# The softmax probabilities of the odd heads are transposed on VectorE instead of TensorE

## The reference

```python
s = jnp.einsum('bkgqd,bksd->bkgqs', qblk, k).astype(jnp.float32) * scale
p = jax.nn.softmax(s, axis=-1).astype(v.dtype)
return jnp.einsum('bkgqs,bksd->bkgqd', p, v)          # self-attention, 8 heads
...
mp = jax.nn.softmax(ms, axis=-1).astype(mv.dtype)
mo = jnp.einsum('bhqm,bhmd->bhqd', mp, mv)             # cross-attention, 4 heads
...
y = (g[:, :, 0] * (y_sgu @ w_br_sgu) + g[:, :, 1] * (y_attn @ w_br_attn) + g[:, :, 2] * (y_mem @ w_br_mem))
x = x + y @ w_out
```

## Time and profile before

| | us |
|---|---|
| median of 3 runs | 2754.28 |
| the profiled execution's own time | 2754.83 |
| its span, first to last instruction | 2753.0 |
| TensorE busy | 2745.2 |
| VectorE busy | 1728.5 |
| ScalarE busy | 1242.9 |
| GpSimd busy | 43.5 |

### The profile page before, as it was taken

One profiled execution on the slowest core, in us unless ns is written; L12 is line 12 of the kernel. 1 busy time (PEld: TensorE's weight loads), 2 busy tenths in 40 slices (PEclk: granted clock), 3 DMA queues, 4 the chain that ended last, 5 costly groups with the idle time before them and its releaser, 6 DMA issues.

```text
span 2753.0 us, 29833 instructions
## 1 busy us (share of the span) xinstructions
PE 2745.2 (100%) x12274; PEld 2276.1 (83%) x12274; DVE 1728.5 (63%) x2110; ACT 1242.9 (45%) x1395; POOL 43.5 (2%) x60
## 2 busy tenths in 40 slices
PE   9999999999999999999999999999999999999999
PEld 7888888888888888888888888888888888888887
DVE  7775555565666576656766755555657665765665
ACT  6545444444444344434454454444444443444343
POOL 0001000000000000000000010000000000000000
PEclk9999999999999999999999999999999999999999
DMA  9544455655555556555555545555555555555554
GB/s 366 188 183 161 180 204 195 212 187 183 185 199 198 192 191 228 191 192 199 190 179 184 181 157 184 194 205 200 178 189 184 199 197 188 197 184 199 186 205 143
DMA packets 77656, 533.76 MB, mean 194 GB/s; under 512 B 8880, under 2 KB 8880, under 8 KB 14928
## 3 DMA queue, kind: packets, MB, share of 16 engines
q1 hardware_dynamic: 75088, 524.32, 53.1%
q0 software_dynamic: 2288, 7.47, 0.9%
q10 hardware_dynamic: 144, 0.06, 0.0%
HBM read 529.72 MB, written 2.10 MB: 193 GB/s over the span
## 4 chain that ended last, share of the span: by engine, by line
PE 99%; DVE 1%; DMA 0%; ACT 0%; DVEq 0%; POOL 0%; issue 0%; SPq 0%; ACTq 0%
PE acc L360 32%; PE acc L362 32%; PE acc L361 32%; PE tr L387 1%; PE tr L451 1%; PE acc L419 1%; PE tr L434 0%; DVE w_lo L906 0%; DMA raw<-weights 0%; PE acc L495 0%; ACT w_hi L610 0%; POOL rows L313 0%; DVE rows L1010 0%; DVE stats L989 0%; DVEq L1058 0%
## 5 line engine op out<-in xcount | busy, mean ns | idle before, releaser
L906 DVE TENSOR_TENSOR w_lo<-raw,w_hi 128x1024 fp32r<-128x1024 f32 x975 | 1191.0, 1225 | 972.9 <-ACT w_hi L610 966.2
L610 ACT ACTIVATE w_hi<-raw 128x1024 fp32r<-128x1024 f32 x975 | 1031.0, 1060 | 1402.5 <-PE acc L362 1396.7
L360 PE MATMUL acc<-w_hi,b_hi 128*128 128x512 f32 x1952 | 764.1, 391 | 1.8 <-DVE b_lo L942 1.7
L360 PE MATMUL acc<-w_hi,a_hi 128*128 128x512 f32 x1952 | 764.3, 392 | 0.0
L362 PE MATMUL acc<-w_hi,a_lo 128*128 128x512 f32 x1952 | 759.9, 389 | 0.0
L362 PE MATMUL acc<-w_hi,b_lo 128*128 128x512 f32 x1952 | 759.8, 389 | 0.0
L361 PE MATMUL acc<-w_lo,b_hi 128*128 128x512 f32 x1952 | 759.5, 389 | 0.0
L361 PE MATMUL acc<-w_lo,a_hi 128*128 128x512 f32 x1952 | 759.4, 389 | 0.0
L360 PEld LDWEIGHTS acc<-w_hi,b_hi 128*128 128x128 f32 x1952 | 366.5, 188 | 78.0 <-DVE b_lo L942 2.1
L362 PEld LDWEIGHTS acc<-w_hi,b_lo 128*128 128x128 f32 x1952 | 366.5, 188 | 76.6
L362 PEld LDWEIGHTS acc<-w_hi,a_lo 128*128 128x128 f32 x1952 | 366.5, 188 | 76.5
(11 more groups left out here) (109 smaller groups left out, 682.0 us busy)
## 6 DMA issues: line engine op xcount, KB each, us to landing
raw<-weights SPq DMA_DIRECT2D x484, 1024.0 KB, 4.8
bias<-bias_in POOLq DMA_DIRECT2D x24, 256.0 KB, 4.5
y<-memT_in SPq DMA_DIRECT2D x16, 256.0 KB, 6.5
raw<-weights SPq DMA_DIRECT2D x7, 512.0 KB, 8.4
rows<-mem_in SPq DMA_DIRECT2D x1, 2048.0 KB, 16.5
x<-xT_in SPq DMA_DIRECT2D x1, 2048.0 KB, 20.8
x<-x_in SPq DMA_DIRECT2D x1, 2048.0 KB, 7.6
out<-x SPq DMA_DIRECT2D x3, 512.0 KB, 7.3
```

Of the source, the lines that this page charges most:

```text
L360: pe.matmul(o, hi[:, kt + k, tok], wh, start=first and k == 0, stop=False)
L610: act.activation(w_hi[:, h % SPLIT_SLOTS, :], raw[:, slot, part * HALF:(part + 1) * HALF], ACT.Copy).then_inc(hi_ready, 1)
L906: dve.tensor_tensor(w_lo[:, h % SPLIT_SLOTS, :], raw[:, slot, part * HALF:(part + 1) * HALF], w_hi[:, h % SPLIT_SLOTS, :].bitcast(F32), AL ...
```

## The change

The transposes of the six odd heads leave TensorE. VectorE gets a function `head_turn` with 16 instructions for a head: for each of four destination quadrants and each of four source quadrants (32 partitions each) one instruction transposes four 32x32 blocks. They go into the same PSUM tile `pT_ps`. `part` is the destination quadrant, `pq` the source quadrant. VectorE runs it in slot 2a+10 behind the split (s = 12, 16, ..., 32, where (s-10)//2 is 1, 3, ..., 11). ScalarE's copy of an odd head moves from slot 2a+11 to slot 2a+12, behind the exponential of head a+2 that stands there; the copy of an even head stays where it was.

```diff
--- before.py
+++ after.py
@@ -422,6 +422,9 @@
 
             def head_turn(a):
 
+                if a % 2 == 1:
+                    n.add("turned")
+                    return
                 pe.wait_ge(prob_ready, n.at("turned", 1))
                 if a == 0:
 
@@ -804,8 +807,10 @@
                         turn_out(qT[:, 4:8, :])
                     if s % 2 == 0 and 0 <= (s - 8) // 2 < N_HEADS:
                         head_exp((s - 8) // 2)
-                    if s % 2 == 1 and 0 <= (s - 11) // 2 < N_HEADS:
+                    if s % 4 == 3 and 0 <= (s - 11) // 2 < N_HEADS:
                         head_pT((s - 11) // 2)
+                    if s % 4 == 2 and 0 <= (s - 12) // 2 < N_HEADS:
+                        head_pT((s - 12) // 2)
                     if s % 2 == 1 and 0 <= (s - 13) // 2 < N_HEADS:
                         head_out((s - 13) // 2)
                 n.add("acc0", NC // 2)
@@ -1066,6 +1071,17 @@
                 dve.wait_ge(exp_done, n.at("inv", 1))
                 dve.reciprocal(inv[:, a % 2, :], den[:, a % 2, :]).then_inc(inv_ready, 1)
                 n.add("inv")
+
+            def head_turn(a):
+
+                dve.wait_ge(prob_ready, n.at("head_base", a + 1))
+                dve.wait_ge(pT_ready, n.at("head_base", a))
+                for part in range(QUADS):
+                    for pq in range(QUADS):
+                        src = prob(a)[pq * SQ:(pq + 1) * SQ, :, :].rearrange("p t (k f i) -> p t k f i", f=QUADS, i=SQ)
+                        to = pT_ps[part * SQ:(part + 1) * SQ, :, :].rearrange("p k (t q i) -> p t k q i", t=TB, q=QUADS)
+                        last = dve.transpose(to[:, :, :, pq, :], src[:, :, :, part, :])
+                last.then_inc(pT_done, 1)
 
             def head_out(a):
                 wait_hi()
@@ -1256,6 +1272,9 @@
                         head_inv((s - 9) // 2)
                     if s % 2 == 1 and 0 <= (s - 13) // 2 < N_HEADS:
                         head_out((s - 13) // 2)
+                    if s % 4 == 0 and 0 <= (s - 10) // 2 < N_HEADS:
+                        head_turn((s - 10) // 2)
+                n.add("head_base", N_HEADS)
 
                 def wait_sig():
                     n.add("sig")
```

## The result

The changed kernel takes 2767.26 us, the median of five runs (2765.33 to 2768.61), against 2754.28 us (2753.79 to 2754.48) before: a ratio of 1.0046, 95% interval 1.0033 to 1.006. It is slower by 13.0 us. The forecast was 2760.8 us in a range of 2751 to 2770, with 0.65 on slower. The profiled execution took 2767.74 us, its span is 2765.9 us, 12.9 us longer than before.

A forecast was written before the change was run, and what follows sets the result against it. TensorE, busy 2745.2 of 2753.0 us, was taken to bound the kernel. Waits of 11.63 us less 5.16 us of removed transposes gave +6.5 us on the median 2754.28: 2760.8 us, range 2751 to 2770.

The forecast's parts named there:

- main case: VectorE's burst of 16 transposes takes 5.0 to 5.6 us, waits as worked out: +3 to +10.5 us, chance 0.55.
- rival C: GpSimd's scaling of the next head meets VectorE's split and becomes TensorE's last wait: +3.8 us, +10.3 in all; chance 0.20.
- B: Size hardly matters to VectorE's transposes: at 0.4625 us each, +32.1 us, 2786.4; chance 0.10 for anything above 0.37 us.
- The gain removed from TensorE: Transposes of 6 odd heads in each of 2 layers leave TensorE, 0.43 us each: 5.16 us gained at most.
- The length of the burst: On VectorE, 16 transposes of 32 partitions by 128 elements per odd head, 0.3295 us each: 5.27 us.
- slope of plain operations: On VectorE, 128 elements cost 416 - 283 = 133 ns, taken off the FFN transpose's 0.4625 us.
- A: VectorE's transposes are short, 0.28 us or less; at 0.231 us, -4.8 us, 2749.5; chance 0.15, including no wait for another reason.
- What becomes late: Behind the burst: split, maximum with negation, exponential, ScalarE's copy, hand-overs, 3.81 us; head 8's transposes on TensorE wait 0.87 us.
- The hand-over to TensorE: From the end of ScalarE's copy of an odd head to TensorE's next transposes: 0.03 us.
- The sum of the waits: TensorE's waits in the attention stage behind the bursts of all odd heads, both layers: 11.63 us.
- What was costed at nothing: Late splits, VectorE's load, weight loads, the even head's copy and head 8's scaling (0.55 us ahead of the copy): no cost.

## Why the prediction was right, and where its sizes were off

**What was right, and what was luck.** The sign, the path and the places of the loss were right: TensorE waits for ScalarE's copy before the transposes of heads 2, 4, 6, 8 and 10 and for VectorE's read before the values of head 11, and the exponential waits for VectorE's negation. The amount was half of what came: +6.5 us forecast, +13.0 measured. That lies above the main case (+3 to +10.5) and above rival C (+10.3), and so does the +11.1 us of the runs whose clock stayed up. The range held it because it was stretched over rival C and part of B, and neither of them happened. That part was luck.

**The gain removed from TensorE.** 5.16 us worked out, 4.9 us measured with the burst cut to one instruction. Right.

**The length of the burst.** 5.27 us worked out, 5.39 from the first transpose to the next split (235.54 to 240.93) and 0.03 before it. The slope of plain operations carried over to the transposes: 323 ns against 330. What was missing is the 0.01 us between two instructions ((5.36 - 16 x 0.323) / 15). Rivals A and B, much shorter and much longer transposes, are out. The estimate of 4.98 us from the 311 ns of the Trainium skill (VectorE: DVE Perf Modes, The three transpose paths) was short by 0.4 us.

**What becomes late.** The step on the chain of split, maximum, exponential and copy was right in order and size: 3.78 us worked out from the end of the burst to the end of the copy (3.81 with the hand-over to TensorE), and from 240.90 to the end of the copy at 244.72, 3.82 us in the trace. The runs with the copy and then the reciprocal moved show each link by taking it away.

**The hand-over to TensorE.** I took 0.03 us, from a pair of rows between TensorE and ScalarE. From the copy's end at 244.72 to the transposes at 244.86 it is 0.14 us. These 0.11 us, the 0.04 of the chain and the 0.15 of the burst make 0.30 us a wait (1.17 measured, 0.87 worked out), 12 times: 3.6 us of the difference.

**The sum of the waits.** 11.63 us worked out. The window from the scores of head 3 to the values of head 11 grew in the profiled execution by (308.47 - 219.24) - (302.38 - 220.06) = 6.91 us in the first layer and by (1687.41 - 1597.61) - (1674.58 - 1592.26) = 7.48 in the second. Adding 5.16 for what was removed and taking off 3.3 for the clock leaves 16.25 us of waits. The view of TensorE's waits agrees: 13.4 + 1.0 us, and 0.16 us more for each of 12. So this term was short by 4.6 us, of which 3.6 is the above. Most of the rest are two waits of the second layer: head 1, where the split ahead of the burst took 1.78 us beside a scaling of GpSimd and not 1.37, and head 7, where VectorE's negation started 0.43 us late, for which the trace gives no cause. The two windows come to 14.4 us; the span grew by 12.9, since TensorE's first stretch and the one between the layers were 0.8 and 0.7 us shorter in that execution.

**What was left out: the clock.** No step of the prediction priced what an idle TensorE does to its own clock. A drop costs 1.63 us, and the profiled execution has two of them, one a layer, 3.3 us in all. The three runs at 0.999 lie 1.9 to 3.2 us above 2765.4; the profiled one lies 2.3 above, less than its two drops, and its other stretches vary by such amounts (the 0.8 and 0.7 us just named). Filling the wait removed the drop in five runs of five, and shortening it did in 11 of 11, while the changed kernel shows it in three of five: so the wait makes the drop likely. Five runs each are few, and those with and without the fill were not in one batch. The wait is neither enough (3.25 us without a drop) nor needed (2 of 52 runs of the kernel before). What decides when the clock falls stays open.

**Rival C, the scaling.** That GpSimd and the split would meet was right, and so was the argument against C, that the split would give way: 1.97 us behind the burst shown, and 1.96 or 1.97 in the others of that layer. The Trainium skill (SBUF — State Buffer, Who interferes with whom) says that the first to issue has the shared ports; the trace agrees, with GpSimd first by 0.15 us and its 1.03 us kept. The scaling ended 0.53 us ahead of the copy, against 0.55 worked out, and that cover was enough; with the copy out of the way it was the next wait.

**What was costed at nothing.** No wait of TensorE for a split or for a weight load appears in the attention stage, so these were rightly free. The split that GpSimd slowed was not quite free: ahead of head 1's burst in the second layer it is the 0.4 us above, and in the two variants with the reciprocal first it moves head 9's burst by 0.7 us, most of the waits of near 1 us that are left there.

## What to carry to other kernels

An engine that is idle for a third of the time (VectorE, 63% busy) could still not take 5.4 us in one piece: what counts is who stands behind the piece in that engine's queue and how soon the bounding engine wants it. Work moved there should be placed behind the small signs that others wait for (here a reciprocal of 0.16 us and a read of 0.4), and the consumer's copy ahead of whatever in its own queue depends on the late engine; with three such moves the same change went from +13 us to -3. Price such a burst by its slack: a burst of 4.0 us cost 0.8 us in all, and above the threshold each microsecond of a burst cost TensorE one, 12 times over.

## What was not expected of the hardware

- TensorE's granted clock fell to 0.50 for about 3 us behind an idle time of 1.94 us, and the matmuls behind it cost 1.63 us more. By the mean granted clock it happened in three executions of five; in the one profiled not behind idle times of 1.0 to 1.6 us in the same execution. With twenty transposes it fell behind idle times of 2.12 and 2.89 us and not behind one of 3.25.
- Four transposes of 32x128 that stay in one source and one destination quadrant took 0.88 us, so with 268 ns each they start about 0.20 us apart and overlap; sixteen that change the source quadrant each time do not overlap and start 0.336 us apart into PSUM ((5.36 - 0.323) / 15) and 0.316 us apart into SBUF ((5.04 - 0.302) / 15).
- The same transpose takes 323 ns into PSUM and 302 ns into SBUF.
